# One core, hybrid decoder layer: the HI projection moved ahead of HQ and HF and done as seven half products

## The chip, the cores and the metric

The kernel runs on one core of a Trainium2 chip. A core has a matrix engine (TensorE, PE in the profile, with its weight loads as PEld), a vector engine (VectorE, DVE), a scalar engine (ScalarE, ACT), GpSimd (POOL) and a queue that mostly issues transfers (SyncE, SP). Each engine works through its own queue in order and waits for the others by semaphores. The metric is device time in microseconds from start to end of one execution, as the median of several.

## The reference

One layer over 512 tokens of width 2048: a norm, one input projection whose columns feed two groups of heads, gated linear attention in each, a norm and a SiLU gate per head, an output projection, and a last norm.

```python
h = rmsnorm(x, norm_w[l])                       # 512 x 2048
proj = h @ w_in[l]                              # 2048 x 7184
gq, gk, gv, gg, glr, hq, hf, hi, hg = jnp.split(proj, offsets, axis=-1)
# widths      512 512 1024 1024 16 1024 1024 1024 1024
log_a = log_sigmoid(glr @ gla_w_up[l] + gla_b_up[l]) / 16
o_a = attention(gq, gk, gv, log_a)              # 4 GLA heads: keys 128, values 256
f = lb + (1.0 - lb) * sigmoid(hf)
o_b = attention(hq, 1.0 - f, hi, log(f))        # 8 HGRN heads: keys 128, values 128
mixed = concat(head_rmsnorm(o_a) * silu(gg), head_rmsnorm(o_b) * silu(hg))
return rmsnorm(x + mixed @ w_out[l])
```

HI is the values of the HGRN heads, as GV is those of the GLA heads. All of it is float32.

## The kernel before

Every float32 product is made of three matmuls: each operand is cut into a high part (`h_hi`, `w_hi`) and the rest (`h_lo`, `w_lo`), and high x high, high x low and low x high are added up. `h` lies in SBUF, transposed, both parts of it. A weight block of 2048 rows and 512 columns is a **group**. It comes in 8 **pieces** of 256 rows (512 KB): SP loads a piece into one of two raw slots (`group` in the sync block, L322), ScalarE copies it to `w_hi` (`split`, L729), VectorE subtracts to `w_lo` (L1045), and TensorE runs 24 matmuls of 512 columns on it (L478), 6 for each of the four banks `main0` to `main3`. `w_hi` and `w_lo` have four slots; both engines work three pieces ahead (LEAD). ScalarE may write a slot when TensorE's `piece_done` says that the piece four back is through. SP asks for a piece when `lo_ok` says that the one two back is split.

The groups come in this order: two for GV (G_V), GQ and GK (G_A), HQ, HF, HQ, HF (G_C), two for HI (G_D), two for GG and two for HG (G_E), and then the output projection (G_F). At the end of a group ScalarE or VectorE empties the four banks (`store`, L888; `values`, L1286; `gates`, L1364), and TensorE's next group waits for that bank by bank with `free`.

Heads are worked on beside the groups. The functions `head` of ScalarE and VectorE make their steps, and dictionaries such as `gla_steps` and `hg_pair` say behind which piece's split a step stands. `head_tasks` in the tensor block does the same for TensorE: behind which of a group's 32 quarter pieces the transposes (T), the six score levels (L), state updates (U), outputs (O) and the mean square (M) stand. One GLA head stands in each of the four G_C groups, two HGRN heads in the second HI group and in each of the next three. So each queue has a fixed order, written out by hand, and a late step on one engine holds up whatever stands behind it there. V and HI lie in the tile `val`, from which ScalarE copies a head's part to `vst` (L768).

The output projection is done as seven half products per pair of column blocks (Strassen's scheme in Winograd's form) instead of eight: `PRODUCTS`, `out_piece` (L688). A half product takes 1024 of the 2048 rows, 256 tokens and 512 columns, its pieces have 12 matmuls. The sums of weight blocks it needs (X1 to X4) are built in DRAM by GpSimd: 16 copies and 16 adding transfers per pair (L450, L458), each held back to one per piece by `pace`, from piece 16 on.

Of the kernel before, what the change touches and what calls it, by code (L numbers as in the profile page):

```python
# [29 lines left out]
P = 128  # L30
# [20 lines left out]
G_V, G_A, G_C, G_D, G_E, G_F, G_END = 0, 2, 4, 8, 10, 14, 18  # L51
# [19 lines left out]
F_N = G_F * NP  # L71
# [49 lines left out]
def hymba_kernel(nc, x, norm_w, w_in, gla_w_up, gla_b_up, gla_norm_w, lb_logits, hgrn_norm_w, w_out,  # L121
                 final_norm_w, out):
    with ExitStack() as ctx:
# [37 lines left out]
        dec = sb("dec", [P, 2])  # L161
# [25 lines left out]
        w_sum = nc.dram_tensor("w_sum", (2, len(XS), QP, P, PK, GW), F32, kind="Internal").ap()  # L187
# [13 lines left out]
        sq_first = ex[0][:, :]  # L201
# [12 lines left out]
        banks = {"X": main[0:2], "Y": main[2:4], "Z": sc, "W": [po, st]}  # L214

# [35 lines left out]
        w_copied = [sem(f"w_copied{i}") for i in range(2 * len(XS))]  # L251
        w_added = [sem(f"w_added{i}") for i in range(2 * len(XS))]
# [27 lines left out]
        kT_ps, kT_ok, v_ok = sem("kT_ps"), sem("kT_ok"), sem("v_ok")  # L280
# [13 lines left out]
        def weight_piece(pair, name, q):  # L294

            if name in XS:
                return w_sum[pair, XS.index(name), q]
            kh, nh = BLOCKS[name]
            r0, c0 = (kh * KT // 2 + q * PK) * P, pair * D // 2 + nh * GW
            return w_out[r0:r0 + PK * P, c0:c0 + GW].rearrange("(k p) n -> p k n", p=P)  # L300

        def wait_bank(eng, G, c):

            if c < 3:
                eng.wait_ge(full, G * 3 + (c + 1))
            else:
                eng.wait_ge(piece_done, G * NP + NP)
# [13 lines left out]
        def _(sp):  # L321
            def group(src, col, G, pieces=range(NP)):  # L322

                for p in pieces:
                    n = NP * G + p
# [19 lines left out]
            with sp.Fori(0, 2) as i:  # L345
                group(w_in, i * GW + C_GQ, i + G_A)
            with sp.Fori(0, 2) as i:
                group(w_in, i * GW + C_HQ, i * 2 + G_C)
                group(w_in, i * GW + C_HF, i * 2 + (G_C + 1))
            with sp.Fori(0, 2) as i:  # L350
                group(w_in, i * GW + C_HI, i + G_D)
# [39 lines left out]
        def _(pool):  # L391
# [42 lines left out]
            step(pool.memset(att[:, :], 0.0))  # L434
            step(pool.memset(kl[1][:, :], 0.0))
# [3 lines left out]
            paced = [2 * NP]  # L439
# [6 lines left out]
            for pair in range(2):  # L446
# [17 lines left out]
        def _(pe):  # L464
# [19 lines left out]
            def group(G, tokens_stationary, tasks=None, pieces=range(NP), before=lambda p: None):  # L484

                tasks = tasks or {}
                for p in pieces:
                    before(p)
                    pe.wait_ge(lo_ok, G * NP + (p + 1))
# [17 lines left out]
            def head_tasks(H, X, nx, at):  # L507
# [39 lines left out]
                def outputs(xx):  # L547
                    def f():
                        pe.wait_ge(sc_ok, H * NL + NL)
                        pe.wait_ge(s_ok, X + (xx + 1))  # L550
                        if nx == 1:
                            pe.wait_ge(norm_ok, X * 1)
                        elif xx:
                            pe.wait_ge(po_read, H + 1)
                        for c in range(NT):
                            cs = slice(c * P, (c + 1) * P)
                            mm = pe.matmul(po[:, cs], vst[vs(xx)][:, c, :], att[:, cs], start=True, stop=(c == 0))  # L557
# [7 lines left out]
                def meansq():  # L565
                    pe.wait_ge(sq_cut, H + 1)
                    ms = ms_bank(nx)
                    pe.matmul(ms[:, :], ones_r[:, :], sq_hi, start=True, stop=False)
                    pe.matmul(ms[:, :], ones_r[:, :], sq_lo[:, :], start=False, stop=True).then_inc(ms_ps, 1)

                def vs(xx):
                    return xx if nx == 2 else at["slot"]
# [79 lines left out]
            with pe.Fori(0, 2) as i:  # L652
                group(i + G_A, False)
            gla_at = dict(slot=0, T=7, L=[9, 11, 12, 14, 16, 17], U=[13, 22], O=[19, 24], M=28)
            with pe.Fori(0, 2) as i:
                for a in range(2):
                    H = i * 2 + a
                    group(i * 2 + (G_C + a), False, head_tasks(H, H * 2, 2, gla_at))

            def hg_pair(m):  # L660

                todo = {}
                for u in range(2):
                    z = 16 * u
                    y = z if u else z + 1
                    at = dict(slot=u, T=z, L=[z + 1] + [y + q for q in (3, 4, 6, 8, 9)], U=[z + 3], O=[y + 10], M=y + 14)
                    todo |= head_tasks(m + (GLA_H + u), m + (8 + u), 1, at)
                return todo

            group(G_D, True)  # L670
            group(G_D + 1, True, hg_pair(0))
# [46 lines left out]
        def _(act):  # L718
            step = Steps(act, a_step)

            def split(G, p):
# [4 lines left out]
                act.wait_ge(raw_in[q % RAW], G * (NP // RAW * 16) + 16 * (q // RAW + 1))  # L726
                if not (isinstance(G, int) and G * NP + q < SPL):
                    act.wait_ge(piece_done, G * NP + (q - SPL + 1))
# [15 lines left out]
            def head(H, X, nx, slot, q_tile):  # L744
# [807 lines left out]
```

## Time and profile before

| | |
|---|---|
| median of 3 runs | 903.39 us (903.21 to 905.16) |
| profiled execution | 903.22 us |
| its span, first to last instruction | 901.5 us |
| TensorE busy | 888.7 us, 99% |
| VectorE busy | 546.5 us, 61% |
| ScalarE busy | 396.4 us, 44% |
| mean granted TensorE clock | 0.998 |
| DMA over the span | 131.30 MB read, 37.75 MB written |

Busy time is the share of the span in which an engine had an instruction in work. Matmuls are pipelined, so one matmul's printed duration is longer than its share of the time. A wait is printed with the engine that ended it. PEclk in the stretches is the granted clock of TensorE, 1.00 being full.

### The profile page before, as it was taken

How to read it: one execution, taken by the hardware profiler on the slowest of the kernel's cores; microseconds unless marked ns; L12 is line 12 of the kernel's file. 1: busy time of each engine (PE TensorE's matmuls, PEld its weight loads, DVE VectorE, ACT ScalarE, POOL GpSimd, SP SyncE). 2: the span in 40 equal slices, each digit the busy share in tenths (PEclk: the TensorE clock that was granted, in tenths of full speed). 3: DMA queues.
4: the chain of work that ended last, by engine and by line, in shares of the span. 5: the costliest groups of instructions: out<-in, count | busy, mean ns of one | idle time of the engine just before them, and what ended most of it. 6: DMA issues, size and time to landing. Idle time of an engine off the chain costs nothing.

```text
span 901.5 us, 12089 instructions
## 1 busy us (share of the span) xinstructions
PE 888.7 (99%) x4371; PEld 740.1 (82%) x4371; DVE 546.5 (61%) x903; ACT 396.4 (44%) x534; POOL 60.6 (7%) x95
## 2 busy tenths in 40 slices
PE   8999999999999999999999999999999999999996
PEld 5787888888888888888888888888888888888885
DVE  6642452227456383753467888787885669555757
ACT  6621521225152442625334545644753555334544
POOL 4000001111111100101111100000000000000000
PEclk9999999999999999999999999999999999999999
DMA  7252256667776654556986633123222527865554
GB/s 265 71 154 80 71 162 193 196 193 161 159 170 139 158 174 140 180 146 162 189 188 126 153 93 84 58 70 93 70 71 71 187 94 245 303 219 189 191 183 186
DMA packets 57557, 136.07 MB, mean 151 GB/s; under 512 B 6117, under 2 KB 6153, under 8 KB 56361
## 3 DMA queue, kind: packets, MB, share of 16 engines
q1 hardware_dynamic: 44050, 101.73, 36.0%
q0 software_dynamic: 11264, 33.56, 17.4%
q10 hardware_dynamic: 2200, 0.22, 0.2%
q8 instruction: 26, 0.43, 0.2%
q14 instruction: 17, 0.14, 0.0%
HBM read 131.30 MB, written 37.75 MB: 188 GB/s over the span
## 4 chain that ended last, share of the span: by engine, by line
PE 95%; DVE 3%; ACT 1%; issue 0%; DMA 0%; DVEq 0%; ACTq 0%
PE main L478 68%; PE main L688 8%; PE sc L688 4%; PE sc L530 3%; PE st L688 2%; PE po L688 2%; PE sc L522 2%; PE po L557 2%; PE st L542 1%; PE po L560 1%; PE main L588 1%; DVE feat L1249 1%; PE st L512 0%; PE st L631 0%; PE st L630 0%
## 5 line engine op out<-in xcount | busy, mean ns | idle before, releaser
L478 PE MATMUL main<-h_hi,w_hi 128*128 128x512 f32 x640 | 259.4, 405 | 0.0
L1045 DVE TENSOR_TENSOR w_lo<-raw,w_hi 128x1024 fp32r<-128x1024 f32 x115 | 140.4, 1222 | 184.9 <-ACT w_hi L729 184.2
L478 PE MATMUL main<-h_hi,w_lo 128*128 128x512 f32 x640 | 250.1, 391 | 0.0
L478 PE MATMUL main<-h_lo,w_hi 128*128 128x512 f32 x640 | 249.7, 390 | 0.0
L729 ACT ACTIVATE w_hi<-raw 128x1024 fp32r<-128x1024 f32 x115 | 121.4, 1057 | 241.0 <-PE main L478 220.3
L478 PEld LDWEIGHTS main<-h_hi,w_lo 128*128 128x128 f32 x640 | 120.1, 188 | 26.6
L478 PEld LDWEIGHTS main<-h_lo,w_hi 128*128 128x128 f32 x640 | 120.5, 188 | 22.2
L478 PEld LDWEIGHTS main<-h_hi,w_hi 128*128 128x128 f32 x640 | 120.5, 188 | 22.1
L478 PE MATMUL main<-w_hi,h_hi 128*128 128x512 f32 x256 | 102.2, 399 | 0.3 <-DVE w_lo L1045 0.3
L478 PE MATMUL main<-w_hi,h_lo 128*128 128x512 f32 x256 | 99.9, 390 | 0.0
L478 PE MATMUL main<-w_lo,h_hi 128*128 128x512 f32 x256 | 99.8, 390 | 0.0
L748 ACT ACTIVATE ex<-ex 128x512 f32<-128x512 f32 (+2 forms) x84 | 52.1, 640 | 57.0 <-DVE ex L1174 39.1
L478 PEld LDWEIGHTS main<-w_hi,h_lo 128*128 128x128 f32 x256 | 48.1, 188 | 10.4
L478 PEld LDWEIGHTS main<-w_hi,h_hi 128*128 128x128 f32 x256 | 48.3, 188 | 10.1 <-DVE w_lo L1045 0.8
L478 PEld LDWEIGHTS main<-w_lo,h_hi 128*128 128x128 f32 x256 | 48.2, 188 | 9.3
L1417 DVE TENSOR_TENSOR w_lo<-feat,w_hi 128x1024 fp32r<-128x1024 f32 x26 | 31.8, 1224 | 28.2 <-ACT w_hi L969 28.0
L969 ACT ACTIVATE w_hi<-raw 128x1024 fp32r<-128x1024 f32 x27 | 28.6, 1060 | 36.4 <-PE main L688 21.6
L1417 DVE TENSOR_TENSOR w_lo<-raw,w_hi 128x1024 fp32r<-128x1024 f32 x27 | 33.0, 1224 | 17.3 <-ACT w_hi L969 17.2
L530 PEld LDWEIGHTS sc<-ql,kl 128*66 128x66 f32 (+2 forms) x384 | 39.0, 162 | 5.2
L969 ACT ACTIVATE w_hi<-feat 128x1024 fp32r<-128x1024 f32 x26 | 27.6, 1060 | 33.7 <-PE main L688 19.7
L450 POOL DMA_DIRECT2D w_sum<-in_w_out x32 | 21.1, 659 | 275.8 <-PE main L478 275.8
L530 PE MATMUL sc<-ql,kl 128*66 128x64 f32 (+2 forms) x384 | 38.8, 244 | 0.0
(244 smaller groups left out, 1209.5 us busy)
## 6 DMA issues: line engine op xcount, KB each, us to landing
raw<-in_w_in SPq DMA_DIRECT2D x112, 512.0 KB, 4.4
w_sum<-in_w_out POOLq DMA_DIRECT2D x48, 512.0 KB, 4.7
w_sum<-w_sum POOLq DMA_DIRECT2D x16, 512.0 KB, 6.1
raw<-w_sum SPq DMA_DIRECT2D x16, 512.0 KB, 3.3
feat<-w_sum SPq DMA_DIRECT2D x16, 512.0 KB, 3.3
raw<-in_w_out SPq DMA_DIRECT2D x14, 512.0 KB, 3.8
feat<-in_x SPq DMA_DIRECT2D x6, 1024.0 KB, 7.3
feat<-in_w_out SPq DMA_DIRECT2D x10, 512.0 KB, 4.3
```

The costliest lines, as they stand in the source:

```text
L450: pool.dma_start(w_sum[pair, j, q], weight_piece(pair, source, q)).then_inc(w_copied[pair * len(XS) + j], 16)
L478: mm = pe.matmul(main[c][:, :], a, b, start=(k == 0 and j == 0), stop=(k == KT - 1 and j == 2))
L522: mm = pe.matmul(sc[l % 2][0:KEYS[l], c % 2 * QW:(c % 2 + 1) * QW], kl[1][:, c * P:c * P + KEYS[l]], eq4[:, c * QW:(c + 1) * QW], start=Tr ...
L530: mm = pe.matmul(sc[l % 2][0:m, c * w:(c + 1) * w], kl[KL[l]][:, c * at_key:c * at_key + m], queries(l)[:, c * w:(c + 1) * w], start=True, ...
L542: mm = pe.matmul(st[:, c * P:(c + 1) * P], kdT[:, c * P:(c + 1) * P], vst[vs(xx)][:, c, :], start=True, stop=True)
L557: mm = pe.matmul(po[:, cs], vst[vs(xx)][:, c, :], att[:, cs], start=True, stop=(c == 0))
L688: mm = pe.matmul(banks[other or bank][a][:, cols], left, right, start=(k == 0 and j == 0 and idx not in ADDS_ON), stop=(k == KT // 2 - 1 a ...
L729: act.activation(w_hi[:, q % SPL, :, :], raw[:, q % RAW, :, :], ACT.Copy).then_inc(hi_ok, 1)
L748: act.activation(dst, src, ACT.Exp, scale=scale).then_inc(exp_ok, 1)
L969: act.activation(w_hi[:, q, :, :], src, ACT.Copy).then_inc(hi_ok, 1)
L1045: dve.tensor_tensor(w_lo[:, q % SPL, :, :], raw[:, q % RAW, :, :], w_hi[:, q % SPL, :, :], ALU.subtract).then_inc(lo_ok, 1)
L1417: dve.tensor_tensor(w_lo[:, q, :, :], src, w_hi[:, q, :, :], ALU.subtract).then_inc(lo_ok, 1)
```

## The change

HI's two groups are gone. In their place, between GK and the first HQ, stand seven half products of 4 pieces with 12 matmuls each (`D_PRODUCTS`), in all eight banks. The sums of `h` that they need (S1, S2, S3) are built by VectorE and ScalarE beside the GQ and GK groups, S4 beside the products themselves, each as 4 slices: three operations on VectorE (`d_build`), a copy on ScalarE (`sum_high`), a subtraction on VectorE (`d_cut`). GpSimd builds the sums of HI's weight blocks first, from piece 1 on, and those of the output weights from piece 60 on. The tile `val` is needed for the sums, so V is written to DRAM (`vd`) during GQ, the HI tiles during and after the products, and ScalarE's queue fetches each head's part (`values`, now transfers). With HI there early, the first two HGRN heads move into the last two G_C groups, beside a GLA head each (`shared_steps`), and the next head's start moves into piece 6 of the group before it. The mean square of a GLA head now uses the bank `po`. Some loops are written out.

```diff
+D_SUMS = {"S1": ("A21", "A22"), "S2": ("S1", "A11"), "S3": ("A11", "A21"), "S4": ("S2", "A12")}
+D_PRODUCTS = [("W", "A12", "B21"), ("X", "A11", "B11"), ("Y", "S1", "X1"), ("X", "S2", "X2"), ("Z", "A22", "X4"),
+              ("X", "S3", "X3"), ("W", "S4", "B22")]
+D_ADDS = (3, 5)
+D_N, ND = G_C * NP, 4 * len(D_PRODUCTS)
...
-            paced = [2 * NP]
+            paced = [1]
-            for pair in range(2):
+            for pair in (2, 0, 1):
+                if pair == 0:
+                    paced[0] = D_N + ND
...
+            for idx, (_, name, _) in enumerate(D_PRODUCTS):
+                if idx in (1, 2):
+                    for c in (2 * idx - 2, 2 * idx - 1):
+                        pe.wait_ge(free[c], G_C)
+                if idx in D_ADDS:
+                    pe.wait_ge(d_out, 1 + D_ADDS.index(idx))
+                for q in range(QP):
+                    if name[0] == "S":
+                        pe.wait_ge(d_low, d_sum(name) + q + 1)
+                    pe.wait_ge(lo_ok, D_N + idx * QP + q + 1)
+                    d_piece(idx, q)
+            pe.wait_ge(d_out, 3)
...
+            alone = dict(T=7, L=[9, 11, 12, 14, 16, 17], U=[13, 22], O=[19, 24], M=28)
+            shared = dict(T=0, L=[1, 4, 5, 7, 9, 10], U=[3, 12], O=[11, 15], M=20)
+            second = dict(T=17, L=[18, 20, 21, 23, 25, 26], U=[20], O=[27], M=31)
+            for h in range(2):
+                group(G_C + h, False, head_tasks(gla_at(h) | alone))
+            for h in range(2):
+                group(G_C + 2 + h, False, both(head_tasks(gla_at(2 + h) | shared), head_tasks(hg_at(0, h) | second)))
-            group(G_D, True)
-            group(G_D + 1, True, hg_pair(0))
...
-                def values():
-                    for xx in range(nx):
-                        col = (X + xx) * P if nx == 2 else (X - 8) * P
-                        act.activation(vst[xx if nx == 2 else slot][:, :, :], val[:, :, bass.ds(col, P)],
-                                       ACT.Copy).then_inc(v_ok, 1)
+                def values():
+                    for xx in range(nx):
+                        to = vst[xx] if nx == 2 else vst_h[slot]
+                        act.dma_start(to[:, :, :], vd[bass.ds(at["R"] + xx, 1), :, :, :].rearrange(
+                            "o p c n -> p (o c) n")).then_inc(values_in(at)[xx if nx == 2 else slot], 16)
...
+            group(G_A, {p: [values_out] * (p == 1) + [sum_high("S1" if p < 4 else "S2", p % 4)] for p in range(NP)},
+                  store(lambda c: 2 * c, SCALE))
+            group(G_A + 1, {p: [sum_high("S3", p)] for p in range(4)}, store(lambda c: 2 * c + 1))
...
+            todo = {13 + 2 * n: [sum_high("S4", n)] for n in range(4)}
+            todo |= {4: [copies(4, 12, "W")], 12: [copies(12, 14, "Y")],
+                     21: [lambda: act.wait_ge(d_low, 16), copies(20, 16, "Y"), copies(20, 18, "Z")], 10: [hi_tiles(1, 12, 0, 0)], 26: [hi_tiles(3, 16, 1, 2), hi_tiles(3, 18, 0, 2)]}
...
+                    step(dve.tensor_tensor(d_t, ah, bh, sign))
+                    step(dve.tensor_tensor(d_u, al, bl, sign))
+                    dve.tensor_tensor(d_v[n % 2], d_t, d_u, ALU.add).then_inc(d_summed, 1)
...
+                    dve.wait_ge(d_high, d_sum(name) + n + 1)
+                    hi, lo = d_operand(name, n)
+                    dve.tensor_tensor(lo, d_v[n % 2], hi, ALU.subtract).then_inc(d_low, 1)
...
+                if nxt:
+                    todo[6] = [f for x in nxt for f in (x["args"], x["ends"], x["early"])]
...
+            def shared_steps(h):
+                g, s = gla_head(2 + h), hg_head(0, h)
+                nxt = gla_head(3) if h == 0 else hg_head(2, 0)
+                ar, sl, cp = g["arg"], g["scale"], g["scores"]
+                ar2, sl2, cp2 = s["arg"], s["scale"], s["scores"]
+                return {0: [g["quads"], ar(4), cp(0), sl(3), ar(5)],
+                        1: [cp(1), cp(2), sl(4), g["states"](0), cp(3), sl(5)],
+                        2: [cp(4), s["args"], cp(5), s["ends"]], 3: [g["states"](1), s["early"], g["cut"]],
+                        4: [s["quads"], ar2(4), cp2(0), sl2(3), ar2(5)],
+                        5: [cp2(1), cp2(2), sl2(4), s["states"](0), cp2(3), sl2(5), g["norm"]],
+                        6: [cp2(4), nxt["args"], cp2(5), nxt["ends"], nxt["early"], s["cut"]], "end": [s["norm"]]}
```

Three places in the queues. The first is ScalarE at the end of the GQ group, before: the last splits, the stores of the four banks, and GK's first split.

```order
L729 ACTIVATE w_hi<-raw 128x1024 [waits piece_done,raw_in1]
L729 ACTIVATE w_hi<-raw 128x1024 [waits piece_done,raw_in0]
L888 ACTIVATE feat<-main 128x512 [waits full] x3
L888 ACTIVATE feat<-main 128x512 [waits piece_done]
L729 ACTIVATE w_hi<-raw 128x1024 [waits piece_done,raw_in1]
```

The same place now; `d_hi_S_56` is a slice of S2, `d_hi_S_57` of S3.

```order
L838 ACTIVATE w_hi<-raw 128x1024 [waits piece_done,raw_in1]
L1015 ACTIVATE d_hi_S_56<-feat 128x512 [waits d_summed]
L838 ACTIVATE w_hi<-raw 128x1024 [waits piece_done,raw_in0]
L1015 ACTIVATE d_hi_S_56<-feat 128x512 [waits d_summed]
L998 ACTIVATE feat<-main 128x512 [waits full] x3
L998 ACTIVATE feat<-main 128x512 [waits piece_done]
L838 ACTIVATE w_hi<-raw 128x1024 [waits piece_done,raw_in1]
L1015 ACTIVATE d_hi_S_57<-feat 128x512 [waits d_summed,v_out]
```

A copy that waits for VectorE (`d_summed`) has moved in between each split and the next, and in front of the stores.

The second is VectorE between the V groups and the first GLA head. Before, from V's copies through GQ and GK to the first HQ group:

```order
L1286 COPY val<-main 128x512 [waits full] x3
L1286 COPY val<-main 128x512 [waits piece_done]
L1045 TENSOR_TENSOR w_lo<-raw,w_hi 128x1024 [waits hi_ok] x8
L1045 TENSOR_TENSOR w_lo<-raw,w_hi 128x1024 [waits piece_done,full,hi_ok]
L1045 TENSOR_TENSOR w_lo<-raw,w_hi 128x1024 [waits hi_ok] x7
L1336 UNCONDITIONAL_BRANCH [waits full,piece_done]
```

Now there are slices in GQ and GK, and then the products. Around their pieces 16 to 18 (`d_hi_S_56` is S2, `d_lo_S_58` the low part of S4):

```order
L1557 TENSOR_TENSOR w_lo<-raw,w_hi 128x1024 [waits hi_ok]
L1510 TENSOR_TENSOR feat<-d_hi_S_56,h_hi 128x512 [waits d_low,piece_done]
L1511 TENSOR_TENSOR feat<-d_lo_S_59,h_lo 128x512 [waits v_step]
L1512 TENSOR_TENSOR feat<-feat 128x512 [waits v_step]
L1557 TENSOR_TENSOR w_lo<-raw,w_hi 128x1024 [waits hi_ok]
L1522 TENSOR_TENSOR d_lo_S_58<-feat,d_hi_S_55 128x512 [waits d_high]
L1557 TENSOR_TENSOR w_lo<-feat,w_hi 128x1024 [waits hi_ok]
L1510 TENSOR_TENSOR feat<-d_hi_S_56,h_hi 128x512 [waits d_low]
```

Where only splits stood, three operations of a slice stand behind one split and its cut behind the next.

The third is ScalarE at the end of an HF group. Before:

```order
L729 ACTIVATE w_hi<-raw 128x1024 [waits piece_done]
L803 ACTIVATE sc<-sc,cst 128x512 [waits ms_ps]
L806 ACTIVATE sc<-sc,cst 128x512 [waits ln_ok]
L305 ISA
L888 ISA [waits full]
L888 ACT_TABLE_LOAD
L888 ACTIVATE feat<-main 128x512
```

And the first HF group now; `vst<-vd` are the transfers of the next head's values, `ex` its exponentials.

```order
L838 ACTIVATE w_hi<-raw 128x1024 [waits piece_done,raw_in1]
L872 DMA vst<-vd 128x512 x2
L859 ACTIVATE ex<-ex 128x384 [waits arg_ok]
L859 ACTIVATE ex<-bcum 128x384 [waits arg_ok]
L859 ACTIVATE ex<-ex 128x512 [waits arg_ok] x2
L838 ACTIVATE w_hi<-raw 128x1024 [waits piece_done,raw_in0]
L913 ACTIVATE po<-po,cst 128x512 [waits ms_ps]
L916 ACTIVATE po<-po,cst 128x512 [waits ln_ok]
L998 ACT_TABLE_LOAD [waits full]
L998 ACTIVATE feat<-main 128x512 [waits hi_out]
L998 ACTIVATE feat<-main 128x512 [waits full] x2
L998 ACTIVATE feat<-main 128x512 [waits piece_done]
```

The next head's four exponentials, which wait for VectorE (`arg_ok`), have moved ahead of the last split and of the stores.

## Rows read from the trace of the kernel before

**Rows 1.** The page: busy time, and the chain that ended last.

```profile
PE 888.7 (99%) x4371; PEld 740.1 (82%) x4371; DVE 546.5 (61%) x903; ACT 396.4 (44%) x534; POOL 60.6 (7%) x95
...
PE 95%; DVE 3%; ACT 1%; issue 0%; DMA 0%; DVEq 0%; ACTq 0%
```

**Rows 2.** Waits, TensorE alone: us in total, times, longest.

```profile
PE main L688 <- DVE w_lo L1417: 0.4, 1, 0.4
```

**Rows 3.** Chain of waits in order of time: start us, us, what.

```profile
99.98 118.37 PE main L478 x522
...
762.73 32.64 PE main L688 x144
```

**Rows 4.** Stretches: one GLA group, one HGRN pair; columns on top.

```profile
core 0: us, PE busy (x) PEld busy (x) DVE busy (x) ACT busy (x) POOL busy (x), PEclk, DMA share, GB/s
207.40:260.60 53.20, 53.20 (x279) 45.04 (x278) 30.54 (x58) 20.89 (x31) 8.28 (x8) 1.00 0.76 150
464.00:522.40 58.40, 58.40 (x324) 49.78 (x323) 47.77 (x101) 27.06 (x42) 6.54 (x8) 1.00 0.66 146
```

**Rows 5.** Timeline, start of the GQ group: start us, us, engine, line.

```profile
121.55 1.06 ACT L729 ACTIVATE w_hi<-raw 128x1024 fp32r<-128x1024 f32 x1 [5.29 <-DMA raw<-in_w_in]
```

**Rows 6.** Timeline, a steady piece of the GQ group.

```profile
158.60 1.06 ACT L729 ACTIVATE w_hi<-raw 128x1024 fp32r<-128x1024 f32 x1 [4.38 <-PE main L478]
...
159.70 1.23 DVE L1045 TENSOR_TENSOR w_lo<-raw,w_hi 128x1024 fp32r<-128x1024 f32 x1 [4.21 <-ACT w_hi L729]
```

**Rows 7.** Lines, shapes apart: busy us, mean ns of one, idle before.

```profile
L888 ACT ACTIVATE feat<-main 128x512 f32<-128x512 f32 x8 | 4.8, 598 | 5.1 <-PE main L478 5.1
```

**Rows 8.** Timeline of VectorE, first GLA group.

```profile
209.08 1.23 DVE L1045 TENSOR_TENSOR w_lo<-raw,w_hi 128x1024 fp32r<-128x1024 f32 x1 [4.64 <-ACT w_hi L729]
210.23 1.22 DVE L1167 TENSOR_TENSOR_SCAN bcum<-reset,feat 128x512 f32<-128x512 uint8 x1
...
212.36 0.69 DVE L1179 SCALAR_TENSOR_TENSOR ex<-kd,bcum 128x512 f32<-128x512 f32 x1
...
215.99 0.68 DVE L1195 TENSOR_TENSOR kl<-feat,ex 128x512 f32<-128x512 f32 x1
216.59 0.68 DVE L1197 TENSOR_TENSOR ql<-feat,ex 128x512 f32<-128x512 f32 x1
...
254.21 1.23 DVE L1045 TENSOR_TENSOR w_lo<-raw,w_hi 128x1024 fp32r<-128x1024 f32 x1 [0.26 <-ACT w_hi L729]
```

**Rows 9.** Timeline of ScalarE, first GLA group.

```profile
213.09 1.15 ACT L748 ACTIVATE ex<-ex 128x512 f32<-128x512 f32 x2
```

**Rows 10.** Timeline of ScalarE, end of an HF group.

```profile
416.49 0.66 ACT L803 ACTIVATE sc<-sc,cst 128x512 f32<-128x512 f32 x1 [0.76 <-PE sc L569]
...
417.86 1.28 ACT L888 ACT_TABLE_LOAD   x1
419.15 2.15 ACT L888 ACTIVATE feat<-main 128x512 f32 x4
```

**Rows 11.** Chain of waits, first GLA group.

```profile
218.35 0.33 PE st L512 x3
...
221.43 0.89 PE sc L530 x8
```

**Rows 12.** Timeline of VectorE, first HGRN pair.

```profile
484.41 0.41 DVE L1162 COPY att<-sc 64x256 f32<-64x256 f32 x1
...
491.20 0.68 DVE L1219 TENSOR_TENSOR sq_lo<-po,lrw 128x512 fp32r<-128x512 f32 x1
```

**Rows 13.** Chain of waits, first HGRN pair.

```profile
485.72 0.45 PE po L557 x4
...
492.77 0.23 PE po L568
```

**Rows 14.** DMA by issuing line: KB each, median us to landing.

```profile
raw<-in_w_in SPq DMA_DIRECT2D x112, 512.0 KB, 4.4
```

**Rows 15.** Timeline: one transfer issued by ScalarE.

```profile
27.24 0.45 ACTq L844 DMA_DIRECT2D bcum<-in_w_in  x1
```

More of the change, by code:

```diff
@@ L651, in _ @@
             group(1, True, {8: [low_rank], 16: [decay_inputs]})
[L652 to L658, printed above, removed]
+            group(G_A, False)
+            group(G_A + 1, False)
@@ new lines, in d_piece @@
+            def d_piece(idx, q):
+                bank, name, _ = D_PRODUCTS[idx]
+                hi, lo = d_operand(name, q)
+                for kk in range(PK):
+                    for a in range(2):
+                        ts = slice(a * P, (a + 1) * P)
+                        for j, (left, right) in enumerate(((hi[:, kk, ts], w_hi[:, q, kk, :]),
+                                                           (hi[:, kk, ts], w_lo[:, q, kk, :]),
+                                                           (lo[:, kk, ts], w_hi[:, q, kk, :]))):
+                            mm = pe.matmul(d_banks[bank][a][:, :], left, right,
+                                           start=(q == 0 and kk == 0 and j == 0 and idx not in D_ADDS),
+                                           stop=(q == QP - 1 and kk == PK - 1 and j == 2), skip_group_check=True)
+                mm.then_inc(piece_done, 1)
@@ new lines, in copies, with f @@
+            def copies(pieces, slot, bank):
+                def f():
+                    act.wait_ge(piece_done, D_N + pieces)
+                    for a in range(2):
+                        mm = act.activation(feat[:, slot + a, :], d_banks[bank][a][:, :], ACT.Copy)
+                    mm.then_inc(d_copied, 1)
+                return f
+            todo = {13 + 2 * n: [sum_high("S4", n)] for n in range(4)}
+            todo |= {4: [copies(4, 12, "W")], 12: [copies(12, 14, "Y")],
+                     21: [lambda: act.wait_ge(d_low, 16), copies(20, 16, "Y"), copies(20, 18, "Z")], 10: [hi_tiles(1, 12, 0, 0)], 26: [hi_tiles(3, 16, 1, 2), hi_tiles(3, 18, 0, 2)]}
@@ new lines, in _ @@
+            for d in range(LEAD, ND + LEAD):
+                if d < ND:
+                    idx, q = d // QP, d % QP
+                    if idx == 0:
+                        act.wait_ge(raw_in[q % RAW], 16 * (D_N // RAW + q // RAW + 1))
+                    else:
+                        act.wait_ge(chain_in[q], 16 * idx)
+                    act.wait_ge(piece_done, D_N + d - SPL + 1)
+                    act.activation(w_hi[:, q, :, :], raw[:, q % RAW, :, :] if idx == 0 else wslot(q),
+                                   ACT.Copy).then_inc(hi_ok, 1)
+                else:
+                    split(G_C, d - ND - LEAD)
+                for f in todo.get(d - LEAD, ()):
+                    f()
@@ new lines, in _ @@
+            for d in range(LEAD, ND + LEAD):
+                if d < ND:
+                    idx, q = d // QP, d % QP
+                    dve.wait_ge(hi_ok, D_N + d + 1)
+                    dve.tensor_tensor(w_lo[:, q, :, :], raw[:, q % RAW, :, :] if idx == 0 else wslot(q),
+                                      w_hi[:, q, :, :], ALU.subtract).then_inc(lo_ok, 1)
+                else:
+                    split(G_C, d - ND - LEAD)
+                for f in todo.get(d - LEAD, ()):
+                    f()
```

319 lines of the change are left out of this document (219 added, 100 removed).

## The prediction

> **What bounds the kernel now.** I read five views in this order. The page first: TensorE is busy 99% of the span, and the chain that ended last is TensorE for 95% [rows 1]. The waits next: past the start, TensorE waits for another engine for 0.7 us in all, and the longest such wait is 0.4 [rows 2]. So every other engine has slack somewhere, and only two things can change the time: how many matmuls TensorE issues, and new waits in its queue. The chain of waits gives the price of a matmul. The 390 to 405 ns that the page prints per matmul is its latency; a gapless run of 522 takes 118.37 us and one of 144 in the output projection 32.64, 0.2268 us each either way [rows 3]. A group of 192 matmuls is 43.54 us, a piece of 24 is 5.44 and a half piece of 12 is 2.72. The stretches show what a head adds to its group of 43.5: 9.7 for a GLA head, 14.9 for two HGRN heads; the granted clock is 1.00 in all [rows 4]. Last the timelines, for how long ScalarE and VectorE take per piece.
>
> **What the change removes.** HI goes from 2 x 192 to 7 x 48 = 336 matmuls. 48 x 0.2268 = 10.9 us leave TensorE. The heads' own matmuls only move: six HGRN heads stay in pairs and two go to the GLA groups. The rest of this part is the search for waits that eat the 10.9.
>
> **Added: end of GQ.** In each piece VectorE now forms a slice of the sums, with ScalarE between its halves. Both queues are in order, so it is a loop: ScalarE's w_hi to VectorE's w_lo 1.10 us [rows 6], w_lo to the next operation 1.15 (209.08 to 210.23), the cut of the last slice 0.60 (start to start without a wait, 215.99 to 216.59), three dependent operations at 0.68 and 0.03 for the semaphore, 2.13 [rows 8], then ScalarE's copy and back to its next w_hi, 0.03 + 0.52. Together 5.53 against a piece of 5.44: no reserve, 0.09 more late each piece. GQ already starts with its w_hi 1.2 late, because the transfer came late [rows 5] (GQ begins at 218.35 - 10.88 - 87.07 = 120.4). The copies of HI blocks now run beside it: I add 0.6, half of what is late already, an estimate. Less the cut that piece 0 doesn't have, w_hi is 1.3 late at piece 1 and 1.8 at piece 7. There ScalarE's stores of the four banks stand behind the last slice: 1.8 + 1.10 + 1.15 + 0.60 + 2.13 + 0.03 = 6.8, 0.52 for the copy, 0.60 for the first store [rows 7] = 7.9 us after the piece began. TensorE wants that bank at 5.44: it waits **2.5**. Bounds: 0.7 with no lateness, 6 if V's four writes, issued by ScalarE in piece 1, don't fit into the 4 us it has free there. One issue takes 0.45 [rows 15], so four take 1.8.
>
> **Added: the half products.** Slots and queue are those of the output projection, where TensorE waits 0.4 once [rows 2]; I take 0.2 for the first product. The trouble is S4, built during pieces 13 to 20. Two pieces cost w_lo 1.15, build 2.13 + 0.03, copy 0.52, w_hi 1.10, w_lo 1.15, cut 0.60 = 6.7 against 5.44, and once 1.25 more for taking two banks. From w_lo of piece 16 to that of piece 23 it is 3 x 6.7 + 1.25 + 4.9 = 26.2 where TensorE needs 19.0: 7.2 late. A w_lo is ready 8.16 - 2.35 = 5.8 before its piece. TensorE waits 1.4. With the first: **1.6**; bounds 0 (the operations overlap as they do without waits) and 5 (every hand-over 0.2 longer).
>
> **Added: the way back into GLA.** Group HQ's third load waits for the last half pieces, since the raw ring has two slots. Counting 4.4 per load [rows 14], w_lo of its fourth piece ends 7.3 after the group starts, and the scan follows; before it came 210.23 - 207.47 = 2.8 after. 4.5 late against the margin of the first scores (218.35 + 3.08 - 217.27 = 4.2) [rows 8, 11]: **0.3**, bounds 0 and 2.
>
> **Added: end of the first HF group.** Here the next GLA head's start is put into piece 6, ahead of ScalarE's last split, the norm's Ln and Exp, the table load and the stores. VectorE's w_lo stands at 254.21, so the scan is at 255.36, its last argument ends 2.8 later at 258.2 [rows 8], two Exps to 259.3 [rows 9], w_hi to 260.3, Ln to table load 1.37, table load to store 1.29 [rows 10], store 0.60: 263.6. TensorE wants the bank at 260.7: **2.9**. Bounds 1 and 4.5. Before, the same stores began at 419.15, 1.2 before the group's end. The Trainium skill, page ScalarE: Activation LUTs, section What ACT_TABLE_LOAD costs, counts a drain of 1380 ns behind a load of 1283. The rows have 1.29 from load to store: no such drain. By the page this term would be 4.3 and the sum 1.4 more; I go by the row.
>
> **Added: two heads in a group.** TensorE's list for the two hosting groups is 43.54 + 9.7 + 7.4 = 60.7 us; VectorE's work is 30.5 - 9.8 for the splits + 47.8 / 2 + 5 = about 50, the share it has in a pair now (47.8 of 58.4). Followed piece by piece, VectorE has the second head's last scores 0.4 us before TensorE wants them, and its squares 0.45 before the mean-square matmul. Now those margins are 0.9 (484.41 + 0.41 to 485.72) and 0.9 (491.20 + 0.68 to 492.77) [rows 12, 13]. I take **0.3**; bounds 0 and 6.
>
> **Hidden.** V and HI through DRAM: 4 MB out and 4 MB back in transfers that nothing awaits within 10 us; ScalarE's 16 copies become issues of the same length. The copies that build the HI sums run beside the V, GQ and GK groups, those for the output weights move from there to the GLA groups and later, one per piece as now. Their cover is the two-slot ring: a load is asked for two pieces ahead, so at 4.4 us to land it has 4 us of slack. A landing over 8.5 us would end that, and each late load would cost what it is over.
>
> **Sum.** -10.9 + 2.5 + 1.6 + 0.3 + 2.9 + 0.3 = -3.3. The profiled execution took 903.22 (span 901.5, 1.7 around it), the median is 903.39: **899.9 us**. Its own range is 896.5 to 902.5 (GQ's wait between 1 and 4, S4's between 0 and 3, the hosting groups' between 0 and 1). 0.2% of the time, about what a measurement of this kernel can tell from no change, is 1.8 us.
>
> **Rivals.**
> - The waits don't appear: hand-overs overlap, and only about 2 us are lost. 894.5. For it: today's queue runs with 0.7 us of waits. Against it: the loop of 5.53 stands on rows.
> - A second wait in the hosting groups: VectorE is 2.5 us later than I counted. Against margins of 0.4 that is 2 us at each of two points in the first hosting group and about 1 in the second: +5, 904.9, no change. For it: some 40 hand-overs in each group, counted at 0.03. Against it: the pair groups run like that without a wait.
> - Slower: ScalarE's DMA issues. It now issues 4 + 8 writes in short rows and 16 reads, in the same queue as the splits. At 2.5 us a write, the four in GQ overrun their 4 us by 6, and because that loop has no reserve, all of it arrives at GQ's end; four more stand in piece 26 of the products, in front of HQ's splits, another 5. 899.9 + 6 + 5 = 911. The gain is gone when a write takes 1.8 us. Against it: 0.45 for a transfer in rows of 64 bytes [rows 15].
> - VectorE spaces all operations as if each waited. [...] The rows show 0.60 between two of 0.68, so it does overlap. With 0.08 more per unwaited operation the GQ loop is 5.7, and 1.2 us are added at GQ's end and 1 in S4: 902.1.
>
> **Chances.** Forecast 0.50, waits absent 0.15, hosting groups 0.15, ScalarE's issues 0.10, spacing 0.10. Faster by over 0.2% needs under 901.6: 0.85 of the forecast, all of the first rival, a quarter of the last, 0.02 from the second: 0.62. Slower needs over 905.2: the issues, a third of the hosting case: 0.15. No change takes 0.23. The range leaves out half of the slower case and the far end of the first: 893.5 to 906.
>
> **What would show it.** TensorE's busy time down by 10.9 less the waits inside; in its waits, ScalarE's store of a bank at the start of GK (2.5) and at the start of the second HQ group (2.9), and w_lo near piece 21 to 23 of the products (1.4). Stretches: GQ 43.5, products 76.2 + 1.6, hosting groups 60.7. I am wrong if either store wait is missing, if a hosting group is over 62, or if a write issued by ScalarE takes over 1 us.

## The result, and the profile after

The changed kernel took a median of **912.12 us** (910.28 to 916.41, 6 runs) against 903.38 (6 runs) for the kernel before: ratio 1.0098, 95% interval 1.0074 to 1.0122. It is 8.7 us slower, where 899.9 was forecast and the range ended at 906. The profiled execution took 913.46, 1.3 over that median; its span is 911.7, 10.2 more than before.

The page of after: busy time and share of span, then the chain that ended last. They answer to [rows 1].

```profile
PE 884.7 (97%) x4323; PEld 735.0 (81%) x4323; DVE 602.3 (66%) x982; ACT 411.7 (45%) x554; POOL 84.9 (9%) x125
...
PE 77%; DVE 10%; ACT 6%; DMA 4%; issue 2%; ACTq 1%; DVEq 0%
```

TensorE's share of the chain fell from 95% to 77%: other engines now release it. TensorE's waits of after (in total, times, longest); [rows 2] had only the last kind:

```profile
PE main L550 <- ACT feat L998: 10.2, 2, 7.4
...
PE st L586 <- DVE kd L1365: 2.4, 1, 2.4
...
PE main L738 <- DVE w_lo L1557: 1.2, 2, 1.0
PE main L796 <- DVE w_lo L1673: 0.4, 1, 0.4
```

L550 is a group's matmul and L998 ScalarE's store: 7.4 at the end of GQ, 2.8 at the end of the first HF group. L586 is the first transpose of HQ's head, L738 the half products. The stretches around these waits in after; columns are length, busy time of PE, PEld, DVE, ACT, POOL (counts), granted clock, DMA share, GB/s. They answer to [rows 4], where every clock was 1.00.

```profile
120.70:164.26 43.56, 43.56 (x193) 35.73 (x191) 26.29 (x36) 10.54 (x13) 7.90 (x8) 1.00 0.98 234
164.26:171.64 7.38, 0.00 (x0) 0.03 (x1) 4.38 (x6) 2.83 (x5) 1.03 (x1) 0.72 0.89 213
171.64:175.00 3.36, 3.36 (x8) 2.68 (x9) 0.96 (x1) 2.26 (x4) 0.00 (x0) 0.50 0.04 14
175.00:180.00 5.00, 5.00 (x17) 3.96 (x17) 2.85 (x5) 0.63 (x1) 0.00 (x0) 0.73 0.33 105
180.00:218.28 38.28, 38.28 (x170) 31.69 (x170) 16.95 (x20) 10.78 (x13) 5.73 (x7) 1.00 0.81 186
218.28:295.70 77.42, 76.21 (x335) 62.52 (x335) 47.27 (x51) 34.42 (x40) 0.81 (x1) 1.00 0.60 190
...
309.43:313.00 3.57, 3.57 (x13) 2.91 (x14) 3.50 (x9) 2.73 (x5) 0.00 (x0) 0.70 1.00 353
...
409.73:413.00 3.27, 3.27 (x10) 2.61 (x11) 1.96 (x3) 3.24 (x5) 0.00 (x0) 0.52 0.94 157
413.00:473.00 60.00, 60.00 (x339) 51.51 (x339) 47.81 (x102) 27.91 (x46) 8.05 (x8) 1.00 0.67 145
```

Read from the top: GQ runs without a gap; 7.38 us idle; then work at clock 0.50, the lower of the two levels (1.2 GHz). GK goes from 171.64 to 218.28, 46.64 us for the matmuls that take 43.54 at full clock: 3.1 more. The products take 76.2 of work and 1.2 of waits. Behind the waits that end at 309.43 and 409.73 the clock is low again; at full clock the same matmuls would have taken 1.7 and 1.6 us less (the first dip reaches to about 314.6). The hosting groups have no gap.

Where the 10.2 us are: -10.9 for the 48 matmuls, +0.3 before GQ, +7.4 and +3.1 at the end of GQ, +1.2 in the products, +2.4 and +1.7 on the way back, +2.8 and +1.6 at the end of HF: 9.6. The other 0.6 I don't place. TensorE's busy time fell only 4.0, because slow matmuls count as busy.

ScalarE's timeline of after in GQ; ACTq rows are its transfer issues, with their length:

```profile
122.65 1.06 ACT L838 ACTIVATE w_hi<-raw 128x1024 fp32r<-128x1024 f32 x1 [6.08 <-DMA raw<-in_w_in]
127.06 0.63 ACT L1015 ACTIVATE d_hi_S<-feat 128x512 fp32r<-128x512 f32 x1 [3.35 <-DVE feat L1512]
127.15 0.42 ACTq L1007 DMA_DIRECT2D vd<-val  x1
...
127.61 9.56 ACTq L1007 DMA_DIRECT2D vd<-val  x3
137.22 0.63 ACT L1015 ACTIVATE d_hi_S<-feat 128x512 fp32r<-128x512 f32 x1 [8.58 <-issue]
...
170.38 0.63 ACT L1015 ACTIVATE d_hi_S<-feat 128x512 fp32r<-128x512 f32 x1 [3.94 <-DVE feat L1512]
170.92 2.04 ACT L998 ACTIVATE feat<-main 128x512 f32<-128x512 f32 x4
```

The four writes of V take 10 us to issue (0.42, 0.64, 1.50 and 7.39), and the next slice's copy starts at 137.22, where the loop of 5.53 would have had it at 132.6. From there to 170.38 are six turns of 5.53: the 4.6 lost are never made up. For the source line of V's writes, min, median and max of an issue in ns, and the time to landing:

```profile
L1007 ACTq DMA_DIRECT2D vd<-val x4: 418/1048/7388, 127.2 to 129.8; - x4
...
DMA to landing us min/median/max: 4.9/13.8/21.6
```

The last issue is the long one. The DMA engines are busy 98% in GQ; by queue, over 120.7 to 164 (packets, MB, share of 16 engines; q0 is GpSimd's, q1 SyncE's, q10 ScalarE's):

```profile
q0 software_dynamic: 1990, 4.11, 54.3%
q1 hardware_dynamic: 2041, 3.92, 24.8%
q10 hardware_dynamic: 4160, 2.10, 18.6%
```

In this stretch q0 carries seven adding transfers and the last of the copies before them.

The way back, from the chain of after:

```profile
296.14 7.41 DMA raw<-in_w_in
...
303.57 1.07 ACT w_hi L838
...
304.74 1.22 DVE w_lo L1220
305.96 1.14 DVE bcum L1343
...
309.43 0.55 PE st L586 x3
```

The fourth load took 7.4 instead of 4.4 [rows 14], beside the HI writes; the scan starts 10.3 after the group, not 7.3. And ScalarE at the end of the first HF group, which answers to [rows 10]:

```profile
405.40 1.05 ACT L838 ACTIVATE w_hi<-raw 128x1024 fp32r<-128x1024 f32 x1
406.35 0.64 ACT L913 ACTIVATE po<-po,cst 128x512 f32<-128x512 f32 x1
407.02 0.66 ACT L916 ACTIVATE po<-po,cst 128x512 f32<-128x512 f32 x1
407.69 1.28 ACT L998 ACT_TABLE_LOAD   x1
408.99 2.06 ACT L998 ACTIVATE feat<-main 128x512 f32<-128x512 f32 x4
```

The chain is the predicted one, 3.6 from the start of w_hi to the start of the stores.

### The profile page after: what moved, and what is told of

Same layout as the page of the kernel before. It is cut to its first block, busy times and chain, and to the rows that moved or that the text cites. A ratio compares the mean times of both kernels' runs of the same rounds, so it can differ in the third digit from the quotient of the medians.

```text
span 911.7 us, 11623 instructions
## 1 busy us (share of the span) xinstructions
PE 884.7 (97%) x4323; PEld 735.0 (81%) x4323; DVE 602.3 (66%) x982; ACT 411.7 (45%) x554; POOL 84.9 (9%) x125
## 4 chain that ended last, share of the span: by engine, by line
PE 77%; DVE 10%; ACT 6%; DMA 4%; issue 2%; ACTq 1%; DVEq 0%
PE main L550 46%; PE main L796 7%; PE sc L796 4%; DMA raw<-in_w_in 4%; PE sc L604 3%; PE main L738 3%; DVE w_lo L1220 2%; ACT w_hi L838 2%; PE st L796 2%; PE po L796 2%; PE sc L596 2%; PE po L631 2%; PE po L634 1%; PE st L616 1%; DVE w_lo L1557 1%
## 5 line engine op out<-in xcount | busy, mean ns | idle before, releaser
L550 PE MATMUL main<-h_hi,w_hi 128*128 128x512 f32 x640 | 263.5, 412 | 10.2 <-ACT feat L998 10.2
L550 PE MATMUL main<-h_hi,w_lo 128*128 128x512 f32 x640 | 252.5, 394 | 0.0
L550 PE MATMUL main<-h_lo,w_hi 128*128 128x512 f32 x640 | 252.0, 394 | 0.0
L1220 DVE TENSOR_TENSOR w_lo<-raw,w_hi 128x1024 fp32r<-128x1024 f32 x102 | 124.6, 1222 | 130.8 <-ACT w_hi L838 129.9
L838 ACT ACTIVATE w_hi<-raw 128x1024 fp32r<-128x1024 f32 x102 | 107.6, 1056 | 173.3 <-PE main L550 131.0
L550 PEld LDWEIGHTS main<-h_hi,w_hi 128*128 128x128 f32 x640 | 121.8, 190 | 32.9 <-issue 11.0
L550 PEld LDWEIGHTS main<-h_hi,w_lo 128*128 128x128 f32 x640 | 121.4, 190 | 27.3
L550 PEld LDWEIGHTS main<-h_lo,w_hi 128*128 128x128 f32 x640 | 122.0, 191 | 22.0
L550 PE MATMUL main<-w_hi,h_hi 128*128 128x512 f32 x128 | 50.4, 394 | 0.5 <-DVE w_lo L1220 0.3
L550 PE MATMUL main<-w_hi,h_lo 128*128 128x512 f32 x128 | 49.9, 390 | 0.0
L550 PE MATMUL main<-w_lo,h_hi 128*128 128x512 f32 x128 | 49.9, 390 | 0.0
L1144 ACT ACTIVATE w_hi<-raw 128x1024 fp32r<-128x1024 f32 x27 | 28.6, 1060 | 36.1 <-PE main L796 21.3
L1673 DVE TENSOR_TENSOR w_lo<-raw,w_hi 128x1024 fp32r<-128x1024 f32 x27 | 33.0, 1224 | 17.0 <-ACT w_hi L1144 16.9
L1015 ACT ACTIVATE d_hi_S<-feat 128x512 fp32r<-128x512 f32 x16 | 10.1, 632 | 68.5 <-DVE feat L1512 59.9
L530 POOL DMA_DIRECT2D w_sum<-w_sum x24 | 19.7, 832 | 138.3 <-PE main L550 133.4
L796 PE MATMUL main<-w_hi,s_hi 128*128 128x512 f32 x80 | 31.1, 389 | 0.0
```

The lines of the kernel that those rows point to most:

```text
L530: pool.dma_start(w_sum[pair, j, q], weight_piece(pair, source, q), accum_op=ALU.add, max_dma_last_dim=4 * PK * GW).then_inc(w_added[pair * ...
L550: mm = pe.matmul(main[c][:, :], a, b, start=(k == 0 and j == 0), stop=(k == KT - 1 and j == 2))
L796: mm = pe.matmul(banks[other or bank][a][:, cols], left, right, start=(k == 0 and j == 0 and idx not in ADDS_ON), stop=(k == KT // 2 - 1 a ...
L838: act.activation(w_hi[:, q % SPL, :, :], raw[:, q % RAW, :, :], ACT.Copy).then_inc(hi_ok, 1)
L1144: act.activation(w_hi[:, q, :, :], src, ACT.Copy).then_inc(hi_ok, 1)
L1220: dve.tensor_tensor(w_lo[:, q % SPL, :, :], raw[:, q % RAW, :, :], w_hi[:, q % SPL, :, :], ALU.subtract).then_inc(lo_ok, 1)
```

## The experiments

The reading after the result: V's writes stop ScalarE in a loop without reserve, three waits and the low clock behind each make up the loss. Rivals: the bytes crowd the loads; the low clock has another cause; the ring's order makes HQ late, not the writes. All edits are to the changed kernel. The runs were timed in three later sessions; before was timed in each of them (903.39, 903.39, 903.38), the changed kernel was not, so its 912.12 is that of the six runs above, and differences to it of 1 or 2 us say little. Each run has one trace, and the waits below are from it.

**v_spread.**

```diff
-            group(G_A, {p: [values_out] * (p == 1) + [sum_high(...)] ...
+            group(G_A, {p: [lambda c=p - 1: values_out(c)] * (1 <= p <= 4) + [sum_high(...)] ...
```

> The four writes of V stay in ScalarE's queue, but one stands in each of GQ's pieces 1 to 4 instead of all four in piece 1. Theory (the issue of a write blocks ScalarE while earlier transfers are still waiting, and the loop of GQ has no reserve): each write has 4 us of idle time to hide in, TensorE's wait for the first store at the end of GQ falls from 7.4 to 2.5 to 3, the stretch of half clock behind it goes, about 904 us. Rival (each issue costs ScalarE some 2.5 us wherever it stands, and pushes the loop): wait 4 to 7, 908 to 912. Rival (the transfers crowd the loads, not the issue): no change, 912.

909.00 (906.06 to 909.72), ratio to before 1.0052 (1.0034 to 1.0070). Its two first writes, TensorE's store waits, and the stretch behind the first:

```profile
126.74 0.42 ACTq L1006 DMA_DIRECT2D vd<-val  x1
...
132.27 0.41 ACTq L1006 DMA_DIRECT2D vd<-val  x1
```

```profile
PE main L550 <- ACT feat L998: 5.5, 2, 2.8
```

```profile
167.00:172.00 5.00, 5.00 (x17) 3.92 (x16) 2.96 (x4) 1.87 (x3) 0.00 (x0) 0.66 0.68 110
```

Each issue is 0.38 to 0.42, though the write ahead had not landed yet (they landed in 6.1 to 9.7 us and stand 5.5 apart). The wait at the end of GQ is 2.7 (2.8 is that of HF), against 2.5 in the prediction. The same bytes move in the same rows over the same stretch, so crowding is not what made the wait 7.4. But the time was expected at 904 and is 5 more: behind the wait of 2.7 is a stretch of low clock too, 5.00 x 0.34 = 1.7 us, and the wait for kd is 2.8 here with 1.6 of low clock behind it.

**v_sp.**

```diff
-            group(w_in, C_GQ, G_A)
+            group(w_in, C_GQ, G_A, range(4))
+            for c in range(4):
+                group(w_in, C_GQ, G_A, range(4 + c, 5 + c))
+                sp.wait_ge(free[c], G_V + 2)
+                sp.dma_start(vd[0:8, :, c, :]..., val[:, c, :]...).then_inc(v_out, 16)
```

> The four writes of V are issued by SyncE's queue, one behind each of the loads 4 to 7 of GQ. Theory (issue on ScalarE): ScalarE's loop never stops, wait at the end of GQ 2.5, no half clock behind it, about 904 us; the same bytes still move. Rival (the bytes themselves crowd the loads, DMA being busy 98% in GQ): 910 to 912. Rival (a blocked issue now holds up SyncE's own loads): w_hi waits for raw in GQ and the wait comes back, 908 or more.

908.59 (907.04 to 911.34), ratio 1.0057 (1.0037 to 1.0076). The longest store wait is 3.1; the loop never stops, but starts 1.8 later than in after (first w_hi at 124.46). The same cure with a little of the last rival. The time is not the 904 of the theory: behind this wait too the low clock costs 1.7.

**v_rows.**

```diff
-                    act.dma_start(vd[0:8, :, c, :].rearrange("x p n -> p x n"), val[:, c, :]...)
+                    act.dma_start(vv[:, c, :], val[:, c, :])
```

> V is written in rows of 4 KB (128 per write instead of 1024 of 512 bytes) to a DRAM tile of its own layout; the reads of a GLA head's part have rows of 512 bytes instead of 2 KB. Order and place of the writes as in the changed kernel. If the number of rows makes the issue block: all four issues under 1 us, wait at the end of GQ 2.5, 904. If the bytes in flight do: the long issue stays, 912. The reads are hidden in both.

910.17 (908.05 to 912.70), ratio 1.0061 (1.0037 to 1.0086). ScalarE's rows:

```profile
127.89 0.85 ACTq L1010 DMA_DIRECT2D vv<-val  x2
...
128.78 2.15 ACTq L1010 DMA_DIRECT2D vv<-val  x2
...
143.23 1.06 ACT L839 ACTIVATE w_hi<-raw 128x1024 fp32r<-128x1024 f32 x1 [3.75 <-DMA raw<-in_w_in]
```

With an eighth of the rows the four issues take 3.0 instead of 10.0 us and fit, though not in the 1 us of the expectation. So the rows count, either their number or their length: the edit changes both. Yet the wait was 6.1, because a load landed late: w_hi starts at 143.23, where the loop would have had it at 139.4 (the 3.75 in brackets is ScalarE's idle time). In this trace crowded loads did act; what made that load late is open. Neither expectation gave both.

**few_adds.**

```diff
-                        pool.dma_start(w_sum[pair, j, q], weight_piece(...), accum_op=ALU.add, ...)
+                        few = slice(0, 4 if pair == 2 else P)
+                        pool.dma_start(w_sum[pair, j, q][few], weight_piece(...)[few], accum_op=ALU.add, ...)
```

> The changed kernel, but GpSimd's 16 adding transfers that build HI's weight sums during GQ and GK move 4 of 128 rows; it leaves out most of those sums, so HI is not the reference's. Theory (a write's issue blocks because its own four writes of 1024 rows fill ScalarE's queue, whatever else moves): one issue still takes 5 us or more, the wait at the end of GQ stays above 5, 910. Rival (it blocks because the DMA engines are saturated by the adds, which take 54% of them): all four issues under 4 us together, wait 2.5, 904; then moving the adds is the cure as well.

906.93 (903.10 to 908.47), ratio 1.0025 (1.0012 to 1.0039). GQ's stretch and the three last issues:

```profile
120.70:164.00 43.30, 43.23 (x191) 35.49 (x189) 28.52 (x38) 12.13 (x15) 6.72 (x8) 1.00 0.55 164
```

```profile
127.77 3.94 ACTq L1008 DMA_DIRECT2D vd<-val  x3
```

With DMA at 0.55 instead of 0.98, the same four writes take 4.4 us and the longest store wait is 3.2. The rival comes close on the issues (under 4 expected) and less so on the wait (2.5) and the time (904); the low clock behind the wait costs 2.9 here. So the long issue needs both: writes of many short rows right behind each other (here the third and fourth took 1.44 and 1.81, in after 1.50 and 7.39), and DMA engines busy with other transfers. That the issue waits for the writes ahead to drain fits all four kernels, but no row shows the queue itself.

**stores_first.**

```diff
-            group(G_A, {... for p in range(NP)}, store(...))
+            group(G_A, {... for p in range(NP - 1)} | {"end": [sum_high("S2", 3)]}, store(...))
```

> ScalarE's copy of the last slice of S2 stands behind the four stores of GQ's banks instead of ahead of them; the V writes are as in the changed kernel. Theory: the store no longer waits for the slice's three operations and copy, so the wait at the end of GQ falls from 7.4 to about 3, and with it most of the half clock (3.1): 905. If the wait had another cause (VectorE's backlog or the loads), the wait stays above 6 and the time at 912.

907.15 (903.97 to 909.74), ratio 1.0035 (1.0021 to 1.0048). The issues are long as before (9.89 for three), the longest wait is 3.0: taking the last slice away from in front of the stores cuts it as much as spreading the writes did. The wait needed both, the lost time and the slice.

**fill.**

```diff
             group(G_A, False)
+            for k in range(30):
+                pe.matmul(st[0:2 * LOWRANK, :], lrw[:, k % KT, :], h_hi[:, k % KT, :], start=True, stop=True)
             group(G_A + 1, False)
```

> The changed kernel with 30 matmuls of 512 columns (6.8 us) into an unused bank, put into TensorE's queue between the GQ and the GK group, where it waits 7.4 us for ScalarE's store; their result is not used. Theory (the idle time is what lowers the clock behind it): the wait shrinks to under 1 us of idle, GK still starts at the same time, but at clock 1.00, and takes 43.5 instead of 46.6 us: 909, 3 us under the changed kernel. Rival (the half clock comes from the work ahead, not from the idle time): the clock is still 0.50 for 3 us and the time 912. Rival (the wait is TensorE's own lateness): the time grows by the filler, 915 or more.

911.45 (909.33 to 913.35), ratio 1.0091 (1.0067 to 1.0114). TensorE's rows, then the stretches:

```profile
163.84 7.08 PE L727 MATMUL st<-h_hi,lrw 128*32 128x512 f32 x30
171.41 0.47 PE L550 MATMUL main<-h_hi,w_hi 128*128 128x512 f32 x1 [0.49 <-ACT feat L1000]
```

```profile
167.00:172.00 5.00, 4.51 (x21) 2.15 (x19) 3.05 (x5) 1.85 (x4) 0.00 (x0) 1.00 0.82 198
172.00:176.00 4.00, 4.00 (x19) 3.33 (x18) 2.19 (x3) 1.68 (x3) 0.00 (x0) 1.00 0.00 1
```

GK starts at the same time as in after, and runs at clock 1.00 from its first matmul. Nothing else was changed, so the low clock came from TensorE's idle time. The medians differ by only 0.7 of the 3 expected, inside the spread of both; in the profile of fill the wait for kd on the way back happened to be 3.7.

**args5.**

```diff
-                    todo[6] = [f for x in nxt for f in (x["args"], x["ends"], x["early"])]
+                    todo[5] = todo[5] + [f for x in nxt for f in (x["args"], x["ends"])]
+                    todo[6] = [x["early"] for x in nxt]
```

> In the first HF group VectorE makes the next head's scan and arguments at the end of piece 5, ahead of its split of piece 6, so ScalarE's exponentials in piece 6 no longer wait for them; the rest is the changed kernel. Theory (the store at the end of that group is late because the next head's chain stands ahead of it): the 2.8 wait is at most 0.5, and the clock behind it stays at 1.00: 908 (912.1 less 2.8 and 1.4). Rival (Ln, Exp and table load alone make it late): the wait stays above 1.3, 910.5. Rival (VectorE's split of piece 6 comes later and TensorE waits for w_lo instead): 912.

910.39 (908.13 to 916.50), ratio 1.0097 (1.0060 to 1.0134): the time alone says nothing. In the trace:

```profile
PE main L550 <- ACT feat L998: 9.8, 2, 8.5
```

So 1.3 are left of 2.8, on the edge between the first reading and the second: half of this wait is the head's chain, half Ln, Exp and table load. No low clock follows, but in five of ten traces none follows the full wait of 2.8 either (see the end of this section). GQ's wait, not touched here, is 8.5; it varies from 7.3 to 8.8 between traces.

**hi_later and ring.**

```diff
-            ..., 26: [hi_tiles(3, 16, 1, 2), hi_tiles(3, 18, 0, 2)]}
+            todo[3] = [hi_tiles(3, 16, 1, 2)]                 # in HQ's list
+            todo[4] = [hi_tiles(3, 18, 0, 2)] + todo[4]
```

```diff
+                    if isinstance(G, int) and G == G_C and p < RAW:
+                        sp.wait_ge(lo_ok, D_N + ND - SPL + 1 + p)
```

> The four HI writes that stand in ScalarE's queue behind HQ's first split (0.4 to 0.9 us each) move into pieces 3 and 4 of the HQ group. Theory (the write traffic beside HQ's loads makes them land in 7.4 instead of 4.4 us): loads land in 4.5, the transposes' wait for kd falls from 2.4 to under 1: 910. Rival (the ring's order sets it, the third and fourth load are asked too late whatever moves beside them): wait 2.0 or more, 912.

> SyncE asks for HQ's first two pieces as soon as the raw slots are free in the last product (two pieces earlier); the HI writes stay. Theory (the loads' order): the third and fourth load start 3 to 4 us earlier, w_lo of HQ's fourth piece ends about 3.5 us after the group starts, the wait for kd is under 0.5: 909.5. Rival (the HI writes beside them): wait still 2 or more, 912.

hi_later 910.05 (2 runs), ring 908.64 (3 runs). Their wait for kd, in this order:

```profile
PE st L586 <- DVE kd L1367: 0.9, 1, 0.9
```

```profile
PE st L588 <- DVE kd L1367: 0.5, 1, 0.5
```

In the nine traces of kernels without these edits (after among them) it is 1.6 to 3.7. Each edit alone takes most of the wait (in hi_later the fourth load lands in 4.9 us), so neither the writes nor the order of the loads makes it late by itself: the wait needs both. Both rivals, which put all of it on one of the two, fall.

**gq_both.** v_spread and stores_first together.

> Both edits at the end of GQ: V's writes one per piece in ScalarE's queue, and the last slice's copy behind the stores. Theory: w_hi of the last piece ends at 161.4, the stores find their banks 2.4 us before GQ's end, so no wait there at all; GK at clock 1.00. Waits left: 1.2 in the products, 2.4 to 2.8 on the way back, 2.8 at the end of HF, and up to 3.5 of half clock behind the last two: 912.1 - 7.4 - 3.1 = 901.6, not over 904. Rival (something else in GQ and GK, such as DMA engines busy 98%, holds the group): a new wait on w_lo or raw in GK of 2 us or more, 905.

902.49 (899.48 to 906.50, 10 runs), ratio 0.9986 (0.9970 to 1.0002): no difference from before that can be told, and three of the ten runs lie over the 904 that was given as the limit. No wait at the end of GQ and no low clock in GK. The ten runs range over 7 us, and their mean clock with them: 0.998 in the three fastest, 0.993 or 0.994 in the four slowest. Two waits of 2.6 and 2.8 are left; in the profiled run the clock stayed at 1.00 behind both. A wait of that length can bring the low clock and need not.

**best.** All five edits.

> All five edits: V's writes spread, the last slice behind the stores, next head's arguments in piece 5 of HF, HI writes later, HQ's first loads earlier. Theory (the four waits and the half clock behind them are the whole difference): left are 48 matmuls fewer, 1.2 in the products, 0.3 on the way back and 0.5 elsewhere: 903.4 - 10.9 + 2.0 = 894.5. Rival (the edits crowd each other, as the HI writes in HQ's pieces 3 and 4 with the loads): 898 or more.

895.55 (895.38 to 897.03), ratio 0.9916 (0.9902 to 0.9929): faster than both kernels. TensorE's waits past the start:

```profile
PE main L552 <- ACT feat L1000: 1.3, 1, 1.3
PE main L740 <- DVE w_lo L1561: 1.2, 2, 0.9
PE main L798 <- DVE w_lo L1678: 0.4, 1, 0.4
```

Expected was 894.5, with 0.5 where 1.3 is left. The clock is 0.995 to 0.999, and most of the spread of the runs is gone with the waits.

**The low clock over all traces.** The wait at the end of the first HF group is 2.8 in ten of the twelve traces. Behind it the clock stayed at 1.00 in five (v_spread, fill, hi_later, ring, gq_both), cost 1.6 or 1.7 us in four (after, v_sp, v_rows, few_adds) and 3.0 in one (stores_first). Behind the nine waits at the end of GQ it always fell, but the cost does not grow with the wait: 1.7 behind 8.8 us in ring, 2.9 behind 3.2 in few_adds. The rows of ring and few_adds behind GQ's wait, then of stores_first and hi_later behind HF's:

```profile
172.62:177.00 4.38, 4.38 (x12) 3.50 (x13) 1.98 (x3) 2.27 (x4) 0.00 (x0) 0.62 0.02 7
167.17:173.00 5.83, 5.83 (x14) 4.58 (x15) 3.37 (x5) 2.26 (x4) 0.00 (x0) 0.50 0.16 33
403.43:410.00 6.57, 6.57 (x21) 5.30 (x22) 4.71 (x8) 5.81 (x9) 0.00 (x0) 0.54 0.78 161
406.35:410.00 3.65, 3.65 (x20) 3.08 (x21) 1.96 (x3) 3.62 (x6) 0.00 (x0) 1.00 0.92 157
```

The cost of a stretch is its length times what the clock lacks to 1.00. So the same wait in the same place has no fixed price, and much of the spread between runs of one kernel can come from this; only the profiled run of each kernel can be read in this way.

## Why the prediction was wrong, step by step

- **48 matmuls, -10.9**: right. The products' work is 76.2, as 336 x 0.2268 gives, and best keeps 7.8 of the 10.9.
- **End of GQ, 2.5**: the loop was right to the hundredth (5.53), and so, nearly, was the wait once the issues are short (2.7 in v_spread). What failed is "One issue takes 0.45, so four take 1.8". They took 10.0, because the price was taken from a single issue, not from one behind others of its kind. Wait 7.4, over the bound of 6 that was given for writes that don't fit. The prediction itself named a write that takes over 1 us to issue as a sign of being wrong; two of the four did. The rival on ScalarE's issues, at 10%, had this mechanism in GQ, where 2.5 us a write makes the 10.0 that four took. Its 911 lies near 912.12 by luck: it added 6 here and 5 on the way back, with nothing for the clock, where 4.9, 2.1 and 6.4 over the forecast were measured, and the four writes on the way back took 2.4 together.
- **No term for the clock**: [rows 4] show 1.00 because before has no wait past 0.4. In the trace of after the low clock behind the wait of 7.4 costs 3.1, behind those of 2.4 and 2.8 it costs 1.7 and 1.6, 6.4 in all. This is the second error, and it would have stood had every wait been sized right: v_spread has the low clock (0.66) behind its wait at GQ's end, which is about the one that was forecast.
- **The products, 1.6**: 1.2 measured.
- **The way back, 0.3**: 2.4. The 4.4 per load is a median over the kernel before, which has no HI writes; the fourth took 7.4, and hi_later and ring show that it took those writes and the late requests of the ring together. The rival put 5 us there by issue time, but the four issues held up no split (the next w_hi waited for its load); the landing was late, not the issue.
- **End of HF, 2.9**: 2.8. The Trainium skill, page ScalarE: Activation LUTs, section What ACT_TABLE_LOAD costs, has a drain of 1380 ns there; from load to store are 1.30 here too, so the row was the one to go by.
- **Hosting groups, 0.3**: 0, TensorE has no gap in 60 us.
- **The rival of spaced operations**: it has GQ's loop at 5.7; the turns are 5.53, so it falls.

The terms that were off add up: 4.9 at GQ, 6.4 for the clock, 2.1 on the way back, less 0.8 elsewhere, 12.6, against 13.6 between 899.9 and the 913.46 of the profiled execution (12.2 to the median). The place of each forecast wait was right; two prices were taken from stretches that lacked what the change adds, and the clock was taken at 1.00 behind every wait.

## What to carry to other kernels

A transfer's issue has no fixed price: on an engine whose queue is in a loop without reserve, spread writes of many rows, one per turn, and look at the DMA share of the stretch first. Keep what frees a bank ahead of work that can wait. When a kernel that never idles TensorE gets waits of 2 us or more, give each a range for the low clock behind it, here 0 to 3 us and not in proportion to the wait, and expect the runs to scatter.

## What the runs showed of the hardware

- A write of 512 KB in rows of 512 bytes took ScalarE 0.38 to 0.42 us to issue when the one ahead had been issued 5.5 us before and was still in flight, and 7.39 as the fourth right behind three others at a DMA share of 0.98; with a share of 0.55 at most 1.81, and in rows of 4 KB the four together 3.0.
- The granted clock fell to 0.50 behind all nine waits of 2.7 to 8.8 us at the end of GQ, at a cost of 1.7 to 3.1 us that does not follow the length of the wait, and stayed at 1.00 when matmuls of 32 stationary columns filled it. Behind the same wait of 2.8 at the end of HF it fell in five of ten traces; the shortest wait with a low clock behind it was 1.9 (for kd, in stores_first).
